# Reading the moving operand of the three-product matmuls from its two halves in turn

## The chip, the cores and the metric

The kernel runs on one core of one Trainium2 chip. The metric is the device time of one execution in microseconds (us), taken as the median over several runs. A profile is one execution recorded by the hardware profiler; its span goes from the first to the last instruction.

## The reference

A decoder trunk of two layers on a residual stream x of 256 tokens by 1024 channels, all in float32. What the change touches are the big weight products: the feed-forward layers' input and output projections, the combined input projection of the token mixer, the projections of its three branches and its output projection.

```python
def _swiglu(h, w_in, w_out):
    gate, up = jnp.split(h @ w_in, 2, axis=-1)
    return (jax.nn.silu(gate) * up) @ w_out
...
for l in range(DEPTH):
    mod = (c_act @ ada_w[l] + ada_b[l]).reshape(bsz, 3, 3, D_MODEL)
    h = _modulated_norm(x, norm_g[l, 0], mod[:, 0, 0], mod[:, 0, 1])
    x = x + MACARON_WEIGHT * mod[:, 0, 2][:, None, :] * _swiglu(h, ffn1_w_in[l], ffn1_w_out[l])
    h = _modulated_norm(x, norm_g[l, 1], mod[:, 1, 0], mod[:, 1, 1])
    mix = _token_mixer(h, positions, mix_w_in[l], ...)
    x = x + mod[:, 1, 2][:, None, :] * mix
    h = _modulated_norm(x, norm_g[l, 2], mod[:, 2, 0], mod[:, 2, 1])
    x = x + MACARON_WEIGHT * mod[:, 2, 2][:, None, :] * _swiglu(h, ffn2_w_in[l], ffn2_w_out[l])
return _rms_norm(x, final_norm_g)
```

Here D_MODEL is 1024 and the feed-forward width is 2816.

## The kernel before

Activations lie transposed: channels on the 128 partitions, the 256 tokens along the free dimension. So every big product has a block of 128 by 128 weights as the stationary operand (the one that TensorE holds) and a strip of 128 channels by 256 tokens as the moving operand (the one that streams through), and its result is 128 output channels by 256 tokens in PSUM, half a bank.

The products are done in float32r, a rounded form of float32. To keep precision, each float32 operand is split into a rounded high part and the rest as a low part, and a product is taken as three: weights high by activations high, weights high by activations low, weights low by activations high. All three add into the same PSUM place. This is `mm3` (lines 1417 to 1421), and its three matmuls are lines 1419, 1420 and 1421 in the profile. It is called by `in_tile` (input projections), by `out_slot` (output projections) and by the branch projections.

Weights come from memory in slots of 2048 columns per partition. SyncE's queue loads a slot into one of the four places of `raw`; ScalarE rounds it into `wh` (line 547); VectorE subtracts to get `wl` (line 868); TensorE uses the slot and counts `w_used` up, on which ScalarE waits to write that slot's place again. `wh` and `wl` have two places each. The activations' parts are `hh` and `hl` (in the profile h_hi and h_lo), `hidh` and `hidl` (hid_hi, hid_lo) for the feed-forward's hidden values, `yh` and `yl` (y_hi, y_lo) for the branches. Gaps are laid between tensors, so that `wh` and `wl` start 128 bytes past a multiple of 512 bytes, and the activations' parts 64 bytes past one.

Other matmuls don't go through `mm3`: `first_slot` (lines 1431, 1433, 1437) takes a stage's first slot in an order of its own, and `tok_mm` (lines 1479 to 1481) has the activations stationary and the weights moving, in one block with 256 columns and in another with 128. The mixer's small matmuls (heads, transposes at line 1731, the solver at line 1824) are in full float32. `fill` puts `mm3` tiles of the gates' projections between them, so that TensorE has work while the other engines prepare.

The order on each engine is the order in which the code is written; waits on semaphores tie the engines together.

Of the kernel before, what the change touches and what calls it, by code (L numbers as in the profile page):

```python
# [173 lines left out]
def hybrid_trunk(nc, a, per_layer, tally):  # L174
    out_dram = a["out"]
    ctx = ExitStack()
    with ctx:
# [1236 lines left out]
        def _(pe):  # L1414
            M = nc.tensor.matmul

            def mm3(out, wsl, rhs_h, rhs_l, start, stop):

                M(out, wh[(slice(None),) + wsl], rhs_h, start=start, stop=False, skip_group_check=True)  # L1419
                M(out, wh[(slice(None),) + wsl], rhs_l, start=False, stop=False, skip_group_check=True)  # L1420
                return M(out, wl[(slice(None),) + wsl], rhs_h, start=False, stop=stop, skip_group_check=True)  # L1421
# [19 lines left out]
            def in_tile(s, half, b, col, n=P):  # L1441

                for k in range(KD):
                    w0 = (half * KD + k) * n
                    last = mm3(PS[0:n, b, col:col + T], (s % 2, slice(w0, w0 + n)), hh[:, k, :], hl[:, k, :],
                               k == 0, k == KD - 1)
                return last
# [4 lines left out]
            def out_slot(n, s, first, last_, rows, l, o):  # L1452


                def product(k, c, start, stop):
                    w0 = k * D + c * P
                    return mm3(out_block(n, c), (s % 2, slice(w0, w0 + P)), *rows(k), start, stop)

                if last_:

                    split_ready(s, 1, o, l)
                    for c in range(KD):
                        product(0, c, False, False)
                        ins = product(1, c, False, True)
                        if c in (1, 3, 5, 6):
                            ins.then_inc(*one("out_done"))
                    ins.then_inc(*one("w_used"))
                    return
                for k in range(2):
                    split_ready(s, k, o, l)  # L1470
                    for c in range(KD):
                        ins = product(k, c, first and k == 0 and c in (0, 2, 4, 6, 7), False)
                ins.then_inc(*one("w_used"))
# [60 lines left out]
            for l in range(DEPTH):  # L1534
# [168 lines left out]
                def fill(parts):  # L1703


                    for part in range(filled[0], filled[0] + parts):
                        j, half, k0 = part // 4, part // 2 % 2, part % 2 * (KD // 2)
                        s = GATE_IN + j
                        if part % 4 == 0 and j >= 2:
                            pe.wait_ge(*at("gate_ready", j - 1, l))  # L1710
                        if k0 == 0:
                            split_ready(s, half, still, l)
                        for k in range(k0, k0 + KD // 2):
                            w0 = (half * KD + k) * P
                            ins = mm3(PS[:, 5 + j % 2, half * T:(half + 1) * T], (s % 2, slice(w0, w0 + P)), hh[:, k, :],
                                      hl[:, k, :], k == 0, k == KD - 1)
                        if part % 4 == 3:
                            ins.then_inc(*one("w_used"))
                    filled[0] += parts
# [108 lines left out]
                for tt in range(TT):  # L1828
                    n = 7 * tt
# [98 lines left out]
                for kb in range(9):  # L1928
                    n, k = kb // 3, kb % 3
# [7 lines left out]
                    for c in range(KD):  # L1937
                        b = BR_BANKS[n] + c // 2
# [99 lines left out]
```

## Time and profile before

| | |
|---|---|
| median of 3 runs | 1378.35 us (1373.07 to 1393.77) |
| profiled execution, its own time | 1366.5 us |
| its span | 1364.7 us |
| mean granted TensorE clock | 0.997 |
| TensorE busy (matmul) | 1293.5 us, 95% of the span |
| TensorE busy (weight load) | 1258.8 us, 92% |
| VectorE, ScalarE, GpSimd busy | 933.4, 632.6, 239.7 us |

The profile gives a row to every instruction. A matmul instruction has two: a weight load (PEld), and the matmul itself (PE). Rows of matmuls overlap, since the next begins before the one before has ended; what a matmul costs in a dense stretch is therefore the time from one start to the next, not the length of its row.

### The profile page before, as it was taken

To read this page: it belongs to the slowest core of one execution; us is meant where nothing else is said; L and a number is where in the kernel's file an instruction comes from. 1 tells how busy PE (TensorE), PEld (TensorE's weight loads), DVE (VectorE), ACT (ScalarE), POOL (GpSimd) and SP (SyncE) were. 2 spreads that over 40 slices of the span, in tenths; PEclk is the share of its full clock that TensorE was granted. 3 is DMA by queue.
4 is the path that set the end of the run, shared out by engine and by line. 5 is a ranking of instruction groups with operands and counts; after the bars stand their busy time and mean duration, and the time that the engine had idled before them with its cause. 6 is when DMAs were issued, how large, how long until landed. Compare 5 with 4: busy or idle time off the path is not lost.

```text
span 1364.7 us, 30015 instructions
## 1 busy us (share of the span) xinstructions
PE 1293.5 (95%) x12966; PEld 1258.8 (92%) x12966; DVE 933.4 (68%) x1324; ACT 632.6 (46%) x913; POOL 239.7 (18%) x265
## 2 busy tenths in 40 slices
PE   2999999999899999999999999999999999999998
PEld 1999998988789999999999999998879999999997
DVE  6777678676756776666676776776765478667655
ACT  2544445566524455444354443547553344644433
POOL 1233440001020001332013331000103000123300
PEclk9999999999999999999999999999999999999999
DMA  9987975515103746776768887662430175577762
GB/s 362 360 295 281 314 282 189 227 47 216 63 4 137 302 166 248 276 289 236 280 233 291 295 312 262 250 247 66 179 127 4 64 294 185 213 261 295 276 219 93
DMA packets 65137, 298.25 MB, mean 219 GB/s; under 512 B 9218, under 2 KB 10242, under 8 KB 47747
## 3 DMA queue, kind: packets, MB, share of 16 engines
q1 hardware_dynamic: 65026, 296.69, 59.3%
q8 instruction: 81, 1.33, 0.4%
q14 instruction: 30, 0.24, 0.0%
HBM read 295.62 MB, written 1.05 MB: 217 GB/s over the span
## 4 chain that ended last, share of the span: by engine, by line
PE 85%; DVE 7%; ACT 4%; DMA 1%; issue 1%; DVEq 1%; ACTq 0%; SPq 0%
PE PS L1419 24%; PE PS L1420 24%; PE PS L1421 24%; PE PS L1824 3%; DVE wl L868 2%; PE PS L1491 1%; DVE scr L894 1%; PE PS L1640 1%; DVE h_lo L887 1%; DMA raw<-in_ada_w 1%; DVE raw L954 1%; PE PS L1431 1%; PE PS L1437 1%; DMA ada_w_ring<-in_ada_w 1%; PE PS L1480 1%
## 5 line engine op out<-in xcount | busy, mean ns | idle before, releaser
L868 DVE TENSOR_TENSOR wl<-raw,wh 128x1024 fp32r<-128x1024 f32 (+1 forms) x400 | 470.2, 1215 | 288.3 <-ACT wh L547 288.1
L547 ACT ACTIVATE wh<-raw 128x1024 fp32r<-128x1024 f32 (+1 forms) x400 | 396.9, 1039 | 474.2 <-PE PS L1421 430.8
L1419 PE MATMUL PS<-h_hi,wh 128*128 128x256 f32 x2160 | 603.3, 279 | 10.8 <-DVE wl L868 6.6
L1420 PE MATMUL PS<-h_lo,wh 128*128 128x256 f32 x2160 | 598.3, 277 | 0.0
L1421 PE MATMUL PS<-h_hi,wl 128*128 128x256 f32 x2160 | 598.2, 277 | 0.0
L1419 PEld LDWEIGHTS PS<-h_hi,wh 128*128 128x128 f32 x2160 | 406.3, 188 | 16.3 <-issue 10.8
L1420 PEld LDWEIGHTS PS<-h_lo,wh 128*128 128x128 f32 x2160 | 406.7, 188 | 0.2
L1421 PEld LDWEIGHTS PS<-h_hi,wl 128*128 128x128 f32 x2160 | 406.6, 188 | 0.0
L1421 PE MATMUL PS<-hid_hi,wl 128*128 128x256 f32 x704 | 194.3, 276 | 0.0
L1419 PE MATMUL PS<-hid_hi,wh 128*128 128x256 f32 x704 | 194.3, 276 | 0.0
L1420 PE MATMUL PS<-hid_lo,wh 128*128 128x256 f32 x704 | 194.3, 276 | 0.0
L954 DVE SCALAR_TENSOR_TENSOR ada_w_ring<-ada_w_ring,c_row 128x1024 f32<-128x1024 f32 x154 | 186.8, 1218 | 10.8 <-ACT c_row L608 7.0
L1325 POOL CAST hid_hi<-hf 128x256 fp32r<-128x256 f32 x88 | 96.1, 1092 | 366.1 <-DVE hf L937 366.1
L1419 PEld LDWEIGHTS PS<-hid_hi,wh 128*128 128x128 f32 x704 | 132.1, 188 | 0.0
L1420 PEld LDWEIGHTS PS<-hid_lo,wh 128*128 128x128 f32 x704 | 132.1, 188 | 0.0
L1421 PEld LDWEIGHTS PS<-hid_hi,wl 128*128 128x128 f32 x704 | 132.1, 188 | 0.0
L1333 POOL TENSOR_TENSOR scr<-scr 128x256 f32<-128x256 f32 x14 | 11.5, 824 | 383.2 <-ACT scr L565 383.0
L1327 POOL TENSOR_TENSOR hid_lo<-hf,hid_hi 128x256 fp32r<-128x256 f32 x88 | 65.2, 741 | 12.7 <-issue 0.2
L1393 POOL TENSOR_TENSOR rw_m<-scr 128x256 f32<-128x256 f32 x24 | 18.0, 770 | 175.3 <-ACT scr L639 79.6
L1431 PE MATMUL PS<-h_hi,wh 128*128 128x256 f32 x96 | 27.1, 302 | 20.6 <-ACT h_hi L580 20.6
L1407 POOL TENSOR_TENSOR A_X<-A_T,cst 128x384 f32<-128x384 f32 x20 | 23.2, 1175 | 109.1 <-DVE A_T L1185 88.2
L1431 PEld LDWEIGHTS PS<-h_hi,wh 128*128 128x128 f32 x96 | 19.9, 208 | 22.0 <-issue 22.0
(284 smaller groups left out, 1402.3 us busy)
## 6 DMA issues: line engine op xcount, KB each, us to landing
raw<-in_ffn_w_in SPq DMA_DIRECT2D x88, 1024.0 KB, 5.6
ada_w_ring<-in_ada_w SPq DMA_DIRECT2D x154, 512.0 KB, 5.1
raw<-in_mix_w_in SPq DMA_DIRECT2D x46, 1024.0 KB, 6.0
raw<-in_ffn_w_out SPq DMA_DIRECT2D x44, 1024.0 KB, 5.8
raw<-in_branch_w SPq DMA_DIRECT2D x8, 1024.0 KB, 9.5
raw<-in_mix_w_out SPq DMA_DIRECT2D x8, 1024.0 KB, 4.9
raw<-in_ada_w SPq DMA_DIRECT2D x6, 512.0 KB, 10.8
raw<-in_mix_w_in SPq DMA_DIRECT2D x4, 512.0 KB, 3.6
```

The lines of the kernel that those rows point to most:

```text
L547: nc.scalar.activation(wh[:, s % 2, h * n:(h + 1) * n], raw[:, s % 4, h * n:(h + 1) * n], ACT.Copy).then_inc(*one("w_hi"))
L868: V.tensor_tensor(wl[:, s % 2, h * n:(h + 1) * n], raw[:, s % 4, h * n:(h + 1) * n], wh[:, s % 2, h * n:(h + 1) * n].bitcast(F32), ALU.sub ...
L954: V.scalar_tensor_tensor(place, place, 1.0, crow[:, :], ALU.mult, ALU.mult, accum_out=adac[:, col:col + 1]).then_inc(*inc("ada_used"))
L1325: G.tensor_copy(dh, hf[:, j % 2, :])
L1327: G.tensor_tensor(dl, hf[:, j % 2, :], dh.bitcast(F32), ALU.subtract).then_inc(*one("hid_ready"))
L1393: G.tensor_tensor(m[:, c, :], pb[:, e % 2, i, 0:T], pb[:, e % 2, i, 1:T + 1], ALU.subtract).then_inc(*one("shift_d"))
L1407: G.tensor_tensor(X[tt], AT[tt], chunk_mask(LEVELS[b]), ALU.mult).then_inc(*one("X_ready"))
L1419: M(out, wh[(slice(None),) + wsl], rhs_h, start=start, stop=False, skip_group_check=True)
L1420: M(out, wh[(slice(None),) + wsl], rhs_l, start=False, stop=False, skip_group_check=True)
L1421: return M(out, wl[(slice(None),) + wsl], rhs_h, start=False, stop=stop, skip_group_check=True)
L1431: M(ps, wh[:, s % 2, w0:w0 + P], hh[:, k, :], start=(k == 0 and half == 0), stop=False, skip_group_check=True)
L1824: ins = M(PS[half(q), b, o:o + 64], lhs[half(q), par, c, :], rhs[half(q), par, c, :], start=True, stop=True)
```

## The change

`mm3` reorders the 256 columns of its moving operand and of its result. Columns are seen as two halves (a) of four runs (b) of 32 columns (n) each, and are taken in the order b, a, n: run 0 of the first half, run 0 of the second half, run 1 of the first half, and so on. With 4 bytes a column, a run is 128 bytes, and the two halves lie 512 bytes apart. The result is written by the same pattern, so each column lands where it landed before. The stationary operand is read as before. No instruction is added, taken away or moved, and no wait changes; `first_slot`, `tok_mm` and all other matmuls stay as they were.

```diff
--- before.py
+++ after.py
@@ -1414,8 +1414,13 @@
         def _(pe):
             M = nc.tensor.matmul
 
+            def turns(t):
+
+                return t.rearrange("p (a b n) -> p b a n", a=2, n=32)
+
             def mm3(out, wsl, rhs_h, rhs_l, start, stop):
 
+                out, rhs_h, rhs_l = turns(out), turns(rhs_h), turns(rhs_l)
                 M(out, wh[(slice(None),) + wsl], rhs_h, start=start, stop=False, skip_group_check=True)
                 M(out, wh[(slice(None),) + wsl], rhs_l, start=False, stop=False, skip_group_check=True)
                 return M(out, wl[(slice(None),) + wsl], rhs_h, start=False, stop=stop, skip_group_check=True)
```

The changed kernel has the same 7165 rows in TensorE's order as the kernel before, one for one; in the rows of `mm3` the operand's form goes from 128x256 to 128x4x2x32, and its three lines become 1424 to 1426.

## Rows read from the trace of the kernel before

**Rows 1.** The page, part 1: busy time, share of the span, instructions; part 2, the TensorE clock.

```profile
PE 1293.5 (95%) x12966; PEld 1258.8 (92%) x12966; DVE 933.4 (68%) x1324; ACT 632.6 (46%) x913; POOL 239.7 (18%) x265
...
PEclk9999999999999999999999999999999999999999
```

**Rows 2.** The page, part 4: the chain that ended last, by engine and by line.

```profile
PE 85%; DVE 7%; ACT 4%; DMA 1%; issue 1%; DVEq 1%; ACTq 0%; SPq 0%
PE PS L1419 24%; PE PS L1420 24%; PE PS L1421 24%; PE PS L1824 3%; DVE wl L868 2%; PE PS L1491 1%; DVE scr L894 1%; PE PS L1640 1%; DVE h_lo L887 1%; DMA raw<-in_ada_w 1%; DVE raw L954 1%; PE PS L1431 1%; PE PS L1437 1%; DMA ada_w_ring<-in_ada_w 1%; PE PS L1480 1%
```

**Rows 3.** The page, part 5: groups by line; busy, mean ns, idle before and its releaser.

```profile
L1419 PE MATMUL PS<-h_hi,wh 128*128 128x256 f32 x2160 | 603.3, 279 | 10.8 <-DVE wl L868 6.6
...
L1419 PE MATMUL PS<-hid_hi,wh 128*128 128x256 f32 x704 | 194.3, 276 | 0.0
```

**Rows 4.** The same groups for the mixer's y tiles, from all groups by line.

```profile
L1419 PE MATMUL PS<-y_hi,wh 128*128 128x256 f32 x144 | 39.7, 276 | 0.0
```

**Rows 5.** Timeline of the feed-forward stage: start us, us it lasts, engine, line, operands.

```profile
149.91 0.28 PE L1419 MATMUL PS<-h_hi,wh 128*128 128x256 f32 x1
149.91 0.19 PEld L1420 LDWEIGHTS PS<-h_lo,wh 128*128 128x128 f32 x1
150.02 0.28 PE L1420 MATMUL PS<-h_lo,wh 128*128 128x256 f32 x1
150.03 0.19 PEld L1421 LDWEIGHTS PS<-h_hi,wl 128*128 128x128 f32 x1
150.14 0.28 PE L1421 MATMUL PS<-h_hi,wl 128*128 128x256 f32 x1
150.14 0.19 PEld L1419 LDWEIGHTS PS<-h_hi,wh 128*128 128x128 f32 x1
```

**Rows 6.** Ends of the timeline from 150 to 160, TensorE alone, and that window's own row.

```profile
149.80 0.28 PE L1421 MATMUL PS<-h_hi,wl 128*128 128x256 f32 x1
...
160.00 0.28 PE L1421 MATMUL PS<-hid_hi,wl 128*128 128x256 f32 x1
...
150.00:160.00 10.00, 10.00 (x91) 1.00 0.81 281
```

**Rows 7.** Ends of the timeline at the mixer's output projection, TensorE alone, and its window.

```profile
485.16 0.36 PE L1419 MATMUL PS<-h_hi,wh 128*128 128x256 f32 x1 [1.31 <-DVE h_lo L1265]
485.35 0.28 PE L1420 MATMUL PS<-h_lo,wh 128*128 128x256 f32 x1
...
496.19 0.28 PE L1419 MATMUL PS<-h_hi,wh 128*128 128x256 f32 x1
...
485.30:496.30 11.00, 11.00 (x94) 1.00 0.51 191
```

**Rows 8.** Timeline of the value projection with 128 moving columns; 48 instructions from 246.94 on.

```profile
246.94 0.22 PE L1479 MATMUL PS<-wh,h_hi 128*128 128x128 f32 x1
247.00 0.28 PE L1480 MATMUL PS<-wh,h_lo 128*128 128x128 f32 x1
...
252.14 0.28 PE L1481 MATMUL PS<-wl,h_hi 128*128 128x128 f32 x1
```

**Rows 9.** Timeline of nine full-precision transposes of 128 columns, merged in one row.

```profile
324.26 1.15 PE L1731 MATMUL PS<-cst,mla_s 128*128 128x128 f32 x9
...
L1731 PE MATMUL PS<-cst,mla_s 128*128 128x128 f32 x36 | 5.0, 276 | 0.0
```

**Rows 10.** Timeline of the shortest matmuls, 64 columns each, merged in one row.

```profile
374.07 1.58 PE L1824 MATMUL PS<-A_inv,A_X 64*64 64x64 f32 x48
```

**Rows 11.** Waits: who waited for whom, us in total, times, longest.

```profile
ACT wh L547 <- PE PS L1421: 430.8, 141, 4.3
DVE wl L868 <- ACT wh L547: 288.1, 159, 4.7
```

**Rows 12.** Windows: PE, PEld, DVE, ACT, POOL busy (instructions), clock, DMA share, GB/s.

```profile
34.00:68.00 34.00, 31.46 (x259) 31.50 (x260) 25.93 (x44) 17.75 (x25) 7.85 (x8) 1.00 0.95 360
68.00:102.00 34.00, 34.00 (x303) 34.00 (x302) 24.36 (x32) 14.13 (x20) 11.75 (x12) 1.00 0.85 294
```

## The prediction

> **What bounds the kernel now.** I read the page's busy times and clock first [rows 1]: TensorE is busy 95% of the span, its weight loads 92%, no other engine over 68%, and the granted clock is 2.4 GHz almost throughout. The chain of waits says the same in another way: 85% of it is TensorE, and the three lines of `mm3` alone hold 24% each, 72% together [rows 2]. The waits show the other engines behind TensorE and not ahead of it: ScalarE waits 430.8 us for TensorE to give back a place of `wh`, and VectorE's split follows ScalarE [rows 11]. So a nanosecond won or lost per `mm3` matmul goes nearly whole into the time. The exception is the start: from 34 to 68 us the DMA engines are 95% busy at 360 GB/s and only 259 matmuls run, against 303 in the next window of the same length [rows 12].
>
> How many matmuls are they? The groups by line give 2160 on h, 704 on the hidden values and 144 on y for each of the three lines [rows 3, 4], so 3 x 3008 = 9024.
>
> What does one cost? The row's own length, 0.28 us, is of no use, since rows overlap; the distance of starts counts. In the feed-forward stage 91 matmuls start from 149.80 to 160.00 [rows 6]: 10.20 us over 90 distances are 113.3 ns. 9024 x 113.3 ns = 1022 us, three quarters of the span, as the chain says.
>
> **What sets the 113.3 ns** decides everything here, because the change touches only the stream of the moving operand and of the result. In the timeline each weight load starts with, or 0.01 us after, the matmul before it, and the next matmul starts 0.11 us later [rows 5]. So two things run side by side in each interval: 256 moving columns pass, and the next 128 weight columns are loaded. Whichever is later sets the pace. Three stretches tell them apart.
>
> First, `tok_mm` with only 128 moving columns and the same 128 weight columns: matmuls number 2 to 48 start from 247.00 to 252.14 [rows 8], 5.14 us over 46 distances, 111.7 ns. Half as many moving columns save 1.6 ns. That speaks for the weight load as the bound, with the moving stream beside it. (It isn't proof: this form may take more than one clock a column.)
>
> Second, nine float32 transposes take 1.15 us, the last of them about 0.276 us [rows 9]: (1.15 - 0.276) / 8 = 109 ns. It is the shortest pace of a full weight load in this trace, and I take it as the floor: 4.1 ns below `mm3`.
>
> Third, the same `mm3` has a slower pace too. At the mixer's output projection 93 matmuls start from 485.35 to 496.19 [rows 7] (the window's 94, less the one at 485.16): 10.84 us over 92 distances, 117.8 ns, at the same clock. The instructions, tiles and starts of tiles are of the same kind as in rows 6. Something in how the two streams meet costs 4.5 ns more there, and the pace holds for the whole stretch. So the pace is not fixed by counts of columns alone.
>
> By the Trainium skill's page "TensorE: Matmul & The Clock Gate" (Part 2, step 1, on LDWEIGHTS) the moving operand and the weights are read through two independent ports of SBUF, and a weight load takes nothing from a running matmul; by that rule the order in which moving columns are read could change nothing, and both rivals of pace below would have no chance. The two paces of rows 6 and 7 keep me from trusting it fully.
>
> **The change part by part.** Instructions, waits, queue entries and bytes: none added, removed or moved, so nothing of the sum comes from there. The stationary side is as before. What is new in each of 9024 matmuls is seven jumps in the reading address and seven in the writing address, between eight runs of 32 columns, and another order in which the moving stream passes the places of a partition.
>
> The jumps: no row of this trace has a TensorE operand in several runs, so I bound them. From below, nothing beyond the pace itself, for as many columns pass as before. From above, by the shortest matmuls here: 48 of 64 columns in 1.58 us [rows 10], less about 0.22 us for the last, are 28.9 ns each; if every run of 32 columns cost as much as such a matmul, one `mm3` matmul would take 231 ns and the kernel 9024 x 118 ns = 1062 us more. I take nothing, for a run is no instruction and has no weight load or start of its own, and because the moving stream has some room beside the weight load: about the 4.1 ns between 109 and 113.3, or 0.6 ns a jump.
>
> The order: from below, the pace falls to the 109 ns of rows 9: 9024 x 4.1 ns = 37 us less, of which about 1 us is lost in the first 68 us where DMA decides, so 36 us. From above, the pace of rows 7 everywhere: 9024 x 4.5 ns = 41 us more, less what already runs so, about 40 us. I take nothing here either, since rows 8 put the pace on the weight load, whose own order doesn't change. Half of the lower end is a case too: the 111.7 ns of rows 8 would bring 9024 x 1.6 ns = 14 us, 1.1%.
>
> The sum is 0 on the profiled execution's 1366.5 us. That execution lies 11.9 us below the median of the three runs, 1378.35 us; differences are put on the median. Forecast: 1378 us, the pace stays at 113.3 ns.
>
> **The rivals.** A measurement of this kernel can tell about 2%, 27.6 us, from no change; over 9024 matmuls that is 3.06 ns each. Cases A to D:
>
> A, the weight load alone sets the pace: 1378 us, its own range 1363 to 1392 (the half gain of 14 us, or as much lost). 0.45.
>
> B, the moving read disturbs the weight read before, and no longer after. In 256 columns the moving stream goes through 1024 bytes while the weight load goes through 512, so with a plain order it overtakes once a matmul; with the halves in turn both advance by 512 bytes a matmul, and it needn't overtake. If that meeting is the 4.1 ns above the floor, the time is 1378 - 36 = 1342 us. For it: 109, 111.7, 113.3 and 117.8 ns for the same weight load. Against it: rows 8, where half the moving columns still take 111.7 ns. It decides from 110.3 ns down. 0.27.
>
> C, the other side: in turns, the fast stream runs ahead over 128 bytes, jumps back, and passes the weight read up to four times instead of once, at each block of 128 bytes. The pace of rows 7 then becomes the rule in all `mm3` stretches: 1378 + 40 = 1418 us. It decides from 116.4 ns up. For it: that pace exists, and holds once it is there; against it: it is rare now, and I can't say what brings it on. 0.20.
>
> D, the jumps are paid: above the room of 4.1 ns, at more than (4.1 + 3.1) / 7 = 1.0 ns a jump, the time is over 2% longer; at 2 ns a jump the pace is 109 + 14 = 123 ns and the time 1378 + 9024 x 9.9 ns = 1467 us. 0.08. The Trainium skill's page "PSUM — Partial Sum Buffer" (Specifications) says that any access pattern that isn't contiguous slows matmuls significantly, with lines of 8 bytes. Taken as it stands it is this rival. A run of 32 columns fills 16 such lines whole, so only the bare wording speaks against the change; no row here tests it.
>
> That the change doesn't reach the chip's instructions is excluded, since the order of the changed kernel carries the form 4x2x32 at these lines.
>
> **How the numbers follow.** The chances are those of the cases: faster by over 2% 0.27 (B), within 2% 0.45 (A), slower by over 2% 0.28 (C and D). The range for 8 in 10 has to hold A, B and C: from 1378 - 42 (B, with some stretches that are at 117.8 ns brought down too) = 1336 to 1378 + 42 = 1420 us. It leaves out D and the tails of B and C, some 0.12.
>
> **What the profile of the changed kernel would show.** The distance of starts in the feed-forward stage decides: 113 ns for A, 109 to 111 for B, about 118 for C, over 120 for D. In B and C ScalarE's wait for TensorE moves the same way, since ScalarE's own work stays: less of the 430.8 us in B, more in C. The start of weight loads beside matmuls tells which stream is late: if the next load starts with each matmul and the matmul follows it at once, the load still leads; if matmuls start long after their load is done, the moving stream has become the bound. VectorE and ScalarE rows should keep their lengths. The forecast would be wrong if either stream hinders the other in SBUF or PSUM in a way that depends on addresses, in whichever direction.

## The result, and the profile after

The changed kernel takes 1409.83 us (median of 4 runs, 1408.28 to 1410.37) against 1379.21 us (4 runs, 1373.07 to 1393.77): slower by more than the 2% that count as clear. The ratio is 1.0267, with a 95% interval of 1.0218 to 1.0316; ratios here and below leave out slow executions (over 1.5% above the fastest of the same kernel, here the one at 1393.77 us), and the two medians by themselves give 1.0222. The four runs of the changed kernel lie within 2.1 us of each other, those of the kernel before within 20.7; that turned out to be a clue.

The profiled execution took 1408.28 us, 41.8 us more in span than the profiled one before. The page of the changed kernel, part 1, the TensorE clock of part 2, and some groups of part 5:

```profile
span 1406.5 us, 30015 instructions
PE 1338.1 (95%) x12966; PEld 1303.4 (93%) x12966; DVE 933.3 (66%) x1324; ACT 633.9 (45%) x913; POOL 239.9 (17%) x265
...
PEclk9999999999999999999999999999999999999999
...
L1424 PE MATMUL PS<-h_hi,wh 128*128 128x256 f32 x2160 | 612.5, 284 | 7.8 <-DVE wl L868 3.5
L1426 PE MATMUL PS<-h_hi,wl 128*128 128x256 f32 x2160 | 607.5, 281 | 0.0
...
L1424 PEld LDWEIGHTS PS<-h_hi,wh 128*128 128x128 f32 x2160 | 406.8, 188 | 13.5 <-issue 10.1
...
L1424 PE MATMUL PS<-hid_hi,wh 128*128 128x256 f32 x704 | 198.0, 281 | 0.0
```

Against [rows 1, 3]: the same count of instructions, the same clock, VectorE, ScalarE and GpSimd as long as before to within 1.3 us, weight loads of 188 ns as before. TensorE's matmul rows alone are longer, by 4 to 5 ns each.

The timeline of TensorE in the feed-forward stage, first and last row from 150 to 160, and that window's row:

```profile
149.83 0.28 PE L1426 MATMUL PS<-h_hi,wl 128*128 128x256 f32 x1
...
159.93 0.28 PE L1424 MATMUL PS<-h_hi,wh 128*128 128x256 f32 x1
...
150.00:160.00 10.00, 10.00 (x86) 1.00 0.88 315
```

86 starts in place of 91 [rows 6]: 10.10 us over 85 distances are 118.8 ns. Over the whole trace the mean distance of starts within `mm3` is 118.8 ns, before it was 113.7 (the stretches at 113.3, but for the one of [rows 7] at 117.8). 9024 x 5.1 ns = 46 us; the span grew by 42. Part of the rest is in the group's idle time, which fell from 10.8 to 7.8 us: a slower TensorE waits less for weights. ScalarE's wait for TensorE grew, as the prediction said it would if the pace fell back:

```profile
ACT wh L547 <- PE PS L1426: 470.2, 141, 4.5
DVE wl L868 <- ACT wh L547: 325.5, 160, 4.8
```

against 430.8 and 288.1 us [rows 11].

### The profile page after: what moved, and what is told of

Same layout as the page of the kernel before. It is cut to its first block, busy times and chain, and to the rows that moved or that the text cites. A ratio compares the mean times of both kernels' runs of the same rounds, so it can differ in the third digit from the quotient of the medians.

```text
span 1406.5 us, 30015 instructions
## 1 busy us (share of the span) xinstructions
PE 1338.1 (95%) x12966; PEld 1303.4 (93%) x12966; DVE 933.3 (66%) x1324; ACT 633.9 (45%) x913; POOL 239.9 (17%) x265
## 4 chain that ended last, share of the span: by engine, by line
PE 86%; DVE 7%; ACT 3%; DMA 1%; issue 1%; DVEq 1%; ACTq 0%; SPq 0%
PE PS L1424 24%; PE PS L1426 24%; PE PS L1425 24%; PE PS L1829 3%; DVE wl L868 2%; PE PS L1496 1%; DMA ada_w_ring<-in_ada_w 1%; PE PS L1645 1%; PE PS L1442 1%; PE PS L1436 1%; DMA raw<-in_ada_w 1%; PE PS L1438 1%; DVE scr L894 1%; PE PS L1486 1%; PE PS L1485 1%
## 5 line engine op out<-in xcount | busy, mean ns | idle before, releaser
L1424 PE MATMUL PS<-h_hi,wh 128*128 128x256 f32 x2160 | 612.5, 284 | 7.8 <-DVE wl L868 3.5
L1426 PE MATMUL PS<-h_hi,wl 128*128 128x256 f32 x2160 | 607.5, 281 | 0.0
L1425 PE MATMUL PS<-h_lo,wh 128*128 128x256 f32 x2160 | 607.4, 281 | 0.0
L1424 PE MATMUL PS<-hid_hi,wh 128*128 128x256 f32 x704 | 198.0, 281 | 0.0
L1425 PE MATMUL PS<-hid_lo,wh 128*128 128x256 f32 x704 | 198.0, 281 | 0.0
L1426 PE MATMUL PS<-hid_hi,wl 128*128 128x256 f32 x704 | 198.0, 281 | 0.0
L1436 PE MATMUL PS<-h_hi,wh 128*128 128x256 f32 x96 | 27.6, 307 | 20.9 <-ACT h_hi L580 20.9
## 6 DMA issues: line engine op xcount, KB each, us to landing
raw<-in_ada_w SPq DMA_DIRECT2D x6, 512.0 KB, 10.8
```

The lines of the kernel that those rows point to most:

```text
L1436: M(ps, wh[:, s % 2, w0:w0 + P], hh[:, k, :], start=(k == 0 and half == 0), stop=False, skip_group_check=True)
```

## The experiments

All paces below are distances of starts in a dense stretch, worked out as above.

### Reading or writing?

**e1_read** turns only the moving operands, **e2_write** only the result.

```diff
-                out, rhs_h, rhs_l = turns(out), turns(rhs_h), turns(rhs_l)
+                rhs_h, rhs_l = turns(rhs_h), turns(rhs_l)        # e1_read
+                out = turns(out)                                 # e2_write
```

> The changed kernel with only the two moving operands read in turns; results are written in plain order, so that their columns land permuted and the output is another one. The trace of the changed kernel has a start every 118.8 ns in the three-product matmuls, before it was 113.3 to 113.7. Theory READ (the new order of the moving read meets the weight read more often): the pace stays near 118.8 ns and the time near 1408 us. Theory WRITE (the jumps in the result's address cost): the pace falls back to 113.3 to 113.7 ns, the time to about 1367 us. Theory JUMPS (each side's seven jumps cost their share): about 116 ns.

> The other half alone: moving operands read in plain order, results written in runs of 32 columns of two halves in turn, so that columns land permuted and the output is another one. READ: back at 113.3 to 113.7 ns and about 1367 us. WRITE: 118.8 ns and about 1408 us. JUMPS: about 116 ns.

e1_read took 1410.98 us, e2_write 1385.56, the kernel before on the same chip 1372.61 (one run each). The timelines, e1_read from 150 to 160 with its window:

```profile
149.81 0.28 PE L1425 MATMUL PS<-h_lo,wh 128*128 128x256 f32 x1
...
159.90 0.28 PE L1426 MATMUL PS<-h_hi,wl 128*128 128x256 f32 x1
...
150.00:160.00 10.00, 10.00 (x86) 1.00 0.86 298
```

10.09 us over 85 distances, 118.7 ns: reading in turns alone gives the whole loss, as theory READ expected. And e2_write, from 150 to 160 and from 530 to 540:

```profile
150.00:160.00 10.00, 10.00 (x91) 1.00 0.77 277
...
529.78 0.28 PE L1425 MATMUL PS<-h_lo,wh 128*128 128x256 f32 x1
...
539.91 0.28 PE L1424 MATMUL PS<-h_hi,wh 128*128 128x256 f32 x1
...
530.00:540.00 10.00, 10.00 (x87) 1.00 0.85 312
```

`mm3` runs in four long feed-forward stretches of 1536 matmuls each (the expectation further down counts 1534). The first is at the old 113.3 ns (91 starts); the second is at 117.8 ns, 10.13 us over 86 distances, and so are the third and the fourth, each to its end. Both are paces of the kernel before [rows 6, 7]; no stretch is at 118.8. READ had expected 1367 us, and the time is 19 us over that. So e2_write isn't "half the loss", as its 13 us over the run before might suggest: it is the old pair of paces, with more stretches at the slower one. Whether the turned write makes the slower one more likely, this single run can't say; in TensorE alone, below, the write changes nothing.

### How many jumps?

```diff
-                return t.rearrange("p (a b n) -> p b a n", a=2, n=32)
+                return t.rearrange("p (a b n) -> p b a n", a=2, n=64)
```

> The changed kernel with runs of 64 columns in place of 32: three jumps per matmul in place of seven. If each jump costs its share of the 5.1 ns between 113.7 and 118.8, the pace is 113.7 + 5.1 x 3/7 = 115.9 ns and the time 9024 x 2.9 ns = 26 us under 1408. If the order in which the two reads pass each other decides, the pace is no straight line in the number of jumps; with half as many returns of the moving read it could be anywhere from 113 to 119 ns.

e3_n64 took 1387.63 us. Its mean pace was 115.9 ns, just what three of seven jumps should cost. That agreement was false: the trace has no stretch at 115.9, only stretches at 113.3 and at 117.8. Here are the windows of its first and its fourth feed-forward stretch:

```profile
150.00:160.00 10.00, 10.00 (x88) 1.00 0.85 298
1250.00:1260.00 10.00, 10.00 (x91) 1.00 0.74 281
```

So I ran the same kernel twelve times more.

> Halves in turn, in runs of 64 columns, timed in rounds. Its single look gave 1387.6 us with two paces in one trace: 113.3 ns in some dense stretches and 117.8 in others, the long feed-forward stretches of 1534 matmuls among them. The plain order has the same two paces. TWO PACES (a stretch falls into either pace at its start and keeps it to its end, in both kernels): both kernels' runs lie on steps of 1534 x 4.45 ns = 6.8 us over about 1366.5 us, from none to four of them (1366.5, 1373.3, 1380.2, 1387.0, 1393.8), and the ratio is unclear, between 0.995 and 1.015. JUMPS (three jumps cost 26 us in every run): this kernel's runs all lie near 1388 to 1395 us, a ratio of 1.008 to 1.015 with little scatter.

Twelve runs: median 1374.33 us, from 1366.03 to 1387.67; 17 runs of the kernel before beside it: 1374.13, from 1365.34 to 1390.59. The ratio is 1.0015 (0.9975 to 1.0055). Runs of 64 columns cost nothing that these runs can tell, JUMPS is out and TWO PACES fits. The 17 runs of the kernel before lie in heaps: five from 1365.3 to 1367.0, six from 1371.9 to 1374.7, three from 1380.0 to 1381.8, two near 1386, one at 1390.6. The first four heaps lie near the steps of 6.8 us that TWO PACES expects of four feed-forward stretches, each of which falls into one of two paces; the last run, expected at 1393.8, lies 3 us off. The traces agree: with none of the four stretches at 117.8 the profiled executions took 1366.5 us (before) and 1366.61 (the turned one with 64 columns), with three of four 1385.56 (e2_write) and 1387.63 (e3_n64), where 1387.0 is expected. No slower execution of the kernel before itself was traced, so for that kernel it is worked out from times. The changed kernel has a single pace, and its runs lie within 2.1 us.

### TensorE by itself

Does the cost need the rest of the kernel? **m1_pace** has TensorE alone run groups of 96 matmuls, weights high by moving high, high by low, low by high, one form per group:

```python
for W, H in ((wh, hh), (wh, hl), (wl, hh)):
    yield o, W[:, c:c + 128], H[:, k:k + w]
...
for o, w, h in triples(32, 16, 256): mm(o, w, turn(h, 32), **K)  # read only
for o, w, h in triples(32, 16, 256): mm(turn(o, 32), w, h, **K)  # write only
```

The first two arguments are the first columns of the weights and of the moving operand past a multiple of 512 bytes; 32 and 16 columns are the kernel's 128 and 64 bytes. I call the first less the second, in bytes, the distance: 64 in the kernel.

> A measurement by itself, which computes nothing of the reference (it hands the input x back): TensorE alone issues groups of 96 matmuls of the three-product kind, in dense runs with a pause before each, in 25 forms, all of them twice. Weights start 0 to 448 bytes past the moving operand's start modulo 512, in steps of 64, for plain order and for halves in turn; then, at the kernel's places (128 and 64), the moving read alone in turns, the write alone in turns, runs of 64, 16 and 8, and 128 and 512 columns. If the meeting of the two reads in a partition decides, the pace differs between places, and reading alone gives 118.8 ns where writing alone gives 113.3. If the jumps are paid, all eight places give one pace in turns, 118.8 ns, and it rises with the count: runs of 64 about 115.5, of 16 about 125, of 8 above 135. If other engines' work matters, here, with them idle, turned and plain forms agree.

The timeline of m1_pace, the 9th and the 96th matmul of three groups (plain at distance 0, then at the kernel's place reading alone in turns, and writing alone in turns):

```profile
34.04 0.28 PE L89 MATMUL PS<-hh,wl 128*128 128x256 f32 x1
...
44.48 0.28 PE L89 MATMUL PS<-hh,wl 128*128 128x256 f32 x1
...
228.49 0.28 PE L121 MATMUL PS<-hh,wl 128*128 128x256 f32 x1
...
238.83 0.28 PE L121 MATMUL PS<-hh,wl 128*128 128x256 f32 x1
...
240.65 0.28 PE L123 MATMUL PS<-hh,wl 128*128 128x256 f32 x1
...
250.51 0.28 PE L123 MATMUL PS<-hh,wl 128*128 128x256 f32 x1
```

Over 87 distances: 10.44 us are 120.0 ns, 10.34 are 118.9, 9.86 are 113.3. Reading alone has the whole cost and writing alone none, as in the whole kernel. The other forms, in the same way, each the same in both passes to 0.1 ns:

| distance in bytes | 0 | 64 | 128 | 192 | 256 | 320 | 384 | 448 |
|---|---|---|---|---|---|---|---|---|
| plain, ns | 120.0 | 113.3 | 118.7 | 117.8 | 120.0 | 113.3 | 118.7 | 117.8 |
| turns of 32, ns | 119.0 | 118.8 | 120.0 | 120.0 | 118.9 | 118.8 | 120.0 | 120.0 |

At distance 64: turns of 64 columns 113.3, of 16 120.0, of 8 123.4; a price for each jump would have given 115.5, 125 and over 135. So no other engine is needed; the distance of the two operands in a partition and the order of the read set the pace, and both rows repeat after 256 bytes. The change's gain or loss depends on that distance: in TensorE alone, turns of 32 gain 1 ns at 0 and lose 5.5 at 64.

### Distance or absolute place?

> Again TensorE alone, nothing of the reference computed (x is handed back), 43 forms of 96 matmuls each. The first such run gave, in plain order, 120.0, 113.3, 118.7 and 117.8 ns with the weights 0, 64, 128 and 192 bytes past the moving operand's place, the same again from 256 on, and in turns of 32 columns 119.0, 118.8, 120.0 and 120.0. Here the steps are 16 bytes; some forms move the moving operand's place instead of the weights'; 512 columns and stationary blocks of 32 and 64 columns are there as well. MEETING (two reads of one partition hinder each other, by their distance in bytes modulo 256): moving the other operand by d gives what the weights moved by 256 - d gave (64: 117.8, 128: 118.7, 192: 113.3), both moved by 64 gives 120.0, and with a weight load of only 32 columns, plain and in turns cost the same, near 109 ns. ADDRESS (the absolute place of the weights or of the moving operand alone counts): moving the moving operand leaves 120.0 or follows a rule of its own. STREAM (the turned stream is slow by itself): with 32 weight columns it stays at 118.8 against 113.3.

With the moving operand moved instead of the weights (m2_places, plain):

| moving operand moved by | 64 | 128 | 192 | both moved by 64 |
|---|---|---|---|---|
| pace, ns | 117.8 | 118.6 | 113.3 | 120.0 |

That is the row above read at 192, 128, 64 and 0: the distance counts, not the place. In steps of 16 bytes, plain, from 0 to 240: 120.0, 118.3, 118.4, 117.8, **113.3**, 118.8, 118.6, 120.1, 118.7, 120.0, 120.0, 118.1, 117.8, 116.7, 117.8, 117.4. Only 64 gives 113.3. Turns of 64 columns gave 120.0, 113.3, 118.7 and 117.8 at 0, 64, 128 and 192, the plain row again. Turns of 32 repeated the table's 119.0, 118.8 and 120.0, but at 192 they gave 118.7 where m1_pace had 120.0: this one place isn't set by the distance alone.

Other shapes follow other rules. With 512 moving columns the plain pace was 226.8, 233.3, 232.3 and 228.9 ns at 0, 64, 128 and 192, so there 64 is the worst of the four and not the best. With 64 weight columns it was 119.1 ns at distance 64 (120.0 in turns). And with 32 weight columns it was 113.3 ns plain and 118.3 in turns: MEETING had expected about 109 for both, and failed there; STREAM had expected this.

Does the whole kernel follow? **e4_same_place** is the kernel before with the distance at 0, **e6_turn_d32** the changed kernel with the distance at 32.

```diff
-        phase("h_gap", 64)
-        base = (base + 511 - 64) // 512 * 512 + 64
+        phase("h_gap", 128)                              # e4_same_place; 96 in e6_turn_d32
+        base = (base + 511 - 128) // 512 * 512 + 128     # the same
```

> The kernel before, plain order, with the activations' parts (and all that lies in the shared region) moved from 64 to 128 bytes past a multiple of 512, where the weights' parts start too: distance 0 in place of 64. By the run of TensorE alone the plain pace there is 120.0 ns and has no second value: MEETING expects a pace of 120.0 ns in the three-product matmuls and 9024 x (120.0 - 113.7) = 57 us over the profiled 1366.5, about 1423 us. If distance matters only with the other engines idle, the pace stays at 113 to 118 ns, 1367 to 1395 us.

> The changed kernel, halves in turn by 32 columns, with the activations' parts and the shared region moved to 96 bytes past a multiple of 512, so that the weights start 32 bytes further on in place of 64. TensorE alone gave 117.8 ns there against 118.8 at 64. MEETING: a pace of 117.8 ns and 1408.3 - 9024 x 1.0 ns = 1399 us. If the pace were the turns' alone: 118.8 ns and 1408 to 1410 us.

e4_same_place took 1420.18 us (1423 expected), 54 more than the profiled execution before and 46 more than the median of the 17 runs, for two shifted starts and no other edit. Its timeline from 150 to 160:

```profile
149.83 0.28 PE L1419 MATMUL PS<-h_hi,wh 128*128 128x256 f32 x1
...
159.91 0.28 PE L1419 MATMUL PS<-h_hi,wh 128*128 128x256 f32 x1
...
150.00:160.00 10.00, 10.00 (x85) 1.00 0.98 339
```

10.08 us over 84 distances, 120.0 ns, as TensorE alone had it. e6_turn_d32 took 1398.69 us, where 1399 were expected and 1409.83 is the changed kernel: 87 starts from 150 to 160, 10.13 us over 86 distances, 117.8 ns. This kernel too has two paces. Its windows in the first and the second feed-forward stretch:

```profile
150.00:160.00 10.00, 10.00 (x87) 1.00 0.87 327
550.00:560.00 10.00, 10.00 (x88) 1.00 0.46 174
```

The second is at 116.7 ns (10.15 us over 87 distances), and so is the third; that makes 117.2 over the whole trace. TensorE alone hadn't shown 116.7 there, so the close hit of 1399 is in part luck.

### Which stream sets the pace?

> TensorE alone once more, 41 forms of 96 matmuls, nothing of the reference computed. So far the pace depends on the distance of weights and moving operand in bytes, modulo 256, and yet a weight load of only 32 columns (its row 108 ns long in place of 188) left the pace where it was: 113.3 plain, 118.3 in turns. Here the stationary block has 8 columns, at 16 distances plain and four in turns, 32 columns at four and four, and the count of moving columns goes from 128 to 512 with 8 and with 128 weight columns. LOAD LENGTH (the two reads hinder each other as long as both run): with 8 weight columns all distances and both orders come near 109 ns, and 512 columns near 216. LOAD START (one collision at the head of each load, however short): the paces at 8 columns follow those at 128, 120.0, 113.3, 118.7, 117.8. STREAM (the moving read has a pace of its own beyond 2.4 GHz a column): with 8 columns 113.3 at every distance, 119 in turns at every distance, and the time rises by more than 0.417 ns a column from 256 to 512.

Timeline of m3_small_load, the 9th and 96th matmul: 8 weight columns with 128 moving columns, then with 256, plain, at distance 64:

```profile
132.84 0.22 PE L101 MATMUL PS<-hh,wl 128*8 128x128 f32 x1
...
138.06 0.22 PE L101 MATMUL PS<-hh,wl 128*8 128x128 f32 x1
...
149.11 0.28 PE L105 MATMUL PS<-hh,wl 128*8 128x256 f32 x1
...
158.97 0.28 PE L105 MATMUL PS<-hh,wl 128*8 128x256 f32 x1
```

60.0 ns and 113.3 ns. The first number settles [rows 8]: 128 moving columns need only 60 ns, so the 111.7 ns there (m3_small_load has 111.7 again with 128 weight columns) are indeed the weight load. The second overturns what I made of it: 256 moving columns take 113.3 ns with almost no weight load beside them, more than the load's 111.7. No group of 256 moving columns in any run, whatever its weights, was below 113.3, so the 109 ns of [rows 9] weren't to be had in this form; 512 columns took 231.1 (LOAD LENGTH had 216).

The same trace shows that the prediction's sign for the later stream, a load that starts with each matmul, doesn't tell the two apart. Here the load lasts 0.09 us of 0.113, can't be the bound, and starts with the matmul all the same, as in [rows 5]:

```profile
155.12 0.28 PE L105 MATMUL PS<-hl,wh 128*8 128x256 f32 x1
155.12 0.09 PEld L105 LDWEIGHTS PS<-hh,wl 128*8 128x8 f32 x1
155.23 0.28 PE L105 MATMUL PS<-hh,wl 128*8 128x256 f32 x1
```

In turns of 32 with 8 weight columns the paces are 117.8, 116.7, 117.8 and 116.7 ns at 0, 64, 128 and 192. So STREAM held mostly, but not alone: the turned read is slower with hardly a load beside it, and a full load adds 1 to 3 ns. Over all runs, the ten groups in turns of 32 with 8 or 32 weight columns lie between 116.7 and 118.7 ns, while 16 of the 23 plain ones are at 113.3. And the short load isn't harmless: plain with 8 columns was at 113.3 for 12 of 16 distances from 0 to 480 and at 115.6 to 120.0 for the other four. Nor does the rule of 256 bytes hold there: 113.3 ns at 64, 120.0 at 320. The same form at 64, 113.3 here, was at 116.7 in the next run (below). With 8 weight columns there are several paces for one form, so these numbers bound the stream's own share and don't fix it.

### Jumps, or places passed twice?

A turn of 32 columns has seven jumps, and it also goes through each 128 bytes of the 256 twice in a row. **m4_orders** separates the two. "matched" jumps as often, or more, but always to the place modulo 256 bytes that comes next in plain order; "twice" reads one run again before going on.

```python
def matched(t, k, n):
    return t.rearrange("p (s u n) -> p s u n", s=k, n=n)[:, :, 0:4 * k:k, :].rearrange("p s u n -> p u s n")
def twice(t, n):
    return t.rearrange("p (b n) -> p b n", n=n).unsqueeze(2).broadcast_to([P, 128 // n, 2, n])
```

> TensorE alone, 33 forms of 96 matmuls, only the order of the moving read differs, results are written plainly and nothing of the reference is computed. A moving stream with 8 weight columns beside it ran at 113.3 ns plain and 116.7 to 117.8 in turns of 32, so the turned read has a slower pace of its own, to which a full weight load adds 1 to 3 ns. Runs of 64 columns, which are 256 bytes, gave the plain pace at all four distances. PLACE (what counts is the sequence of places modulo 256 bytes that the read goes through): eight runs of 32 and sixteen runs of 16 that jump by whole 256s plus the next place (matched32, matched16) give the plain pace, 113.3 ns at a distance of 64 and 120.0 at 0, whatever the count of jumps; reading one run of 32 twice before going on (twice32) gives what turns of 32 give, 118.8 ns, and twice64 gives 113.3. JUMPS (each jump shorter than 64 columns costs): matched32 is at 118.8, matched16 at 120.0 like turns of 16, and stay32 (eight runs, all at the same place modulo 256) at 118.8 as well.

Timeline of m4_orders at distance 64 with 128 weight columns, 9th and 96th matmul: turns of 32 (L112), matched in eight runs of 32 (L118), matched in sixteen of 16 (L120), each run of 32 twice (L126):

```profile
57.33 0.28 PE L112 MATMUL PS<-hh,wl 128*128 128x256 f32 x1
...
67.67 0.28 PE L112 MATMUL PS<-hh,wl 128*128 128x256 f32 x1
...
94.41 0.28 PE L118 MATMUL PS<-hh,wl 128*128 128x256 f32 x1
...
104.27 0.28 PE L118 MATMUL PS<-hh,wl 128*128 128x256 f32 x1
...
106.10 0.28 PE L120 MATMUL PS<-hh,wl 128*128 128x256 f32 x1
...
115.96 0.28 PE L120 MATMUL PS<-hh,wl 128*128 128x256 f32 x1
...
142.40 0.28 PE L126 MATMUL PS<-hh,wl 128*128 128x256 f32 x1
...
152.74 0.28 PE L126 MATMUL PS<-hh,wl 128*128 128x256 f32 x1
```

118.9, 113.3, 113.3 and 118.9 ns. Fifteen jumps cost nothing if the place modulo 256 bytes goes on as in plain order; seven jumps that repeat the place cost 5.5 ns, and as much when the repeated run is the very same columns. Runs of 64 read twice gave 113.3, staying at one place for all eight runs 120.0, and both matched forms at distance 0 gave 120.0, the plain value there. PLACE held at every form with full weights, and JUMPS is out there. With 8 weight columns it isn't so clean: matched in eight runs of 32 gave 113.3, but in sixteen of 16 120.0, the same as turns of 16, and plain 116.7.

## Why the prediction was wrong

The forecast was 1378 us with the pace unchanged; the time of rival C came true, nearly at its price (1418 forecast, 1410 measured). The stated range, up to 1420, held the result only because C was in it.

**Right.** That `mm3`'s pace decides and TensorE is the bound: 5.1 ns per matmul came back as 42 us of span. That nothing else moves: VectorE's and ScalarE's rows kept their lengths. The count of 9024. That the jumps and the write cost nothing (against D): m1_pace shows it for the write, m4_orders for the jumps of the read with full weights.

**The step that failed** is in "What sets the 113.3 ns": "That speaks for the weight load as the bound, with the moving stream beside it." [rows 8] show what the load needs, 111.7 ns, and it is true that the load sets the pace there (TensorE alone took 111.7 with 128 moving columns, and 60.0 once the load was short). But I had no row for what 256 moving columns need without a load and assumed about 109 ns from full-precision transposes; measured they need 113.3. The stream on which the change works was the later of the two already, by 1.6 ns, and had none of the 4.1 ns of room that the forecast counted on. An order that slows the moving read, to 116.7 or more even with a short load, shows at once.

**Also failed, the step from which A took its weight:** "I take nothing here either, since rows 8 put the pace on the weight load, whose own order doesn't change." The pace of full weights isn't the load's alone: with both orders unchanged, e4_same_place shifted the starts and went from 113.3 to 120.0 ns. Plain order at the kernel's distance of 64 bytes is the one good case among the sixteen distances tried; turning the read leaves it.

**B** rested on the picture that in plain order the moving read overtakes the weight read once a matmul at a cost of 4.1 ns. At the kernel's distance plain order with full weights costs no more than the stream with 8 weight columns (113.3 both), so there was nothing to win. At distance 0, where plain order takes 120.0, turns gain 1 ns in TensorE alone, B's direction but a quarter of its size.

**C's picture and size.** That C came true is in part luck. In its picture the moving read jumps back and passes the weight read up to four times. But the matched orders jump at least as often and cost nothing (113.3), and the turned read is slow with 8 weight columns too. For its size, C took the slower pace of [rows 7], 117.8 ns, for all stretches. The pace is another one, 118.8, so in the profile the loss is 42 us and not 40. In the medians it is 31 us; going by its times, the kernel before has one or more of its feed-forward stretches at 117.8 in most runs, where its profiled execution had none, and I took that for the rule. The pace of [rows 7] was no rare case of the mixer: in e2_write and e3_n64 three of the four long stretches have it.

The Trainium skill's rule of two independent read ports ("TensorE: Matmul & The Clock Gate", Part 2, step 1) isn't what these runs show: shifting where the weights or the moving operand start, with all else kept, moved the pace between 113.3 and 120.0 ns with full weights. The wording of the Trainium skill's page "PSUM — Partial Sum Buffer" (Specifications), that any write which isn't contiguous slows matmuls, isn't borne out either for runs of 32 columns: m1_pace has 113.3 ns with and without.

**Open:** what brings a stretch of the kernel before into 113.3 or 117.8 ns at its start (TensorE alone, after a pause, was at 113.3 all nine times that a group in plain order with full weights ran at distance 64 modulo 256); and the mechanism inside the memory. The runs show, for full weights and 256 columns, a rule in distances modulo 256 bytes and in repeated places; whether it is the two reads that collide, or the stream with itself in part, they show only in so far as the turned read is slow with 8 weight columns too.

## What to carry to other kernels

When a change alters how an operand is read, ask what its stream needs alone, not only which of two parallel streams a trace row seems to show as the later; a few groups of the bare instruction on the idle engine answer that in one run. With float32r matmuls of 128 weight and 256 moving columns, treat the distance between the starts of weights and moving operand modulo 256 bytes as a parameter: it was worth up to 6% of a matmul's pace, and 46 to 54 us in this kernel. Measure it anew for another shape, for with 512 columns the order of the distances was another. Keep reads in an order that goes through those 256 bytes evenly. Before a mean pace is explained by a fraction (three jumps of seven), look whether any stretch has that pace.

## What the runs showed of the hardware

- The pace of 128 by 128 weights with 256 moving float32r columns at 2.4 GHz depends on the distance of the operands' starts modulo 256 bytes: 113.3 ns at 64, 116.7 to 120.1 at the other fifteen steps of 16. In the whole kernel, 64 and 0 are 1366.5 and 1420 us in the profiled executions. With 512 columns, 0 is the best of four distances (226.8 ns) and 64 the worst (233.3).
- 256 moving float32r columns take 113.3 ns at best, with 8 weight columns beside them as with 128; with 8, 128 take 60.0 and 512 take 231.1: about 0.44 to 0.47 ns a column, more than the 0.417 of one column a clock at 2.4 GHz.
- With full weights, the order of the read costs by the places modulo 256 bytes that it repeats, not by its jumps (118.8 ns against 113.3 at distance 64); the write in runs of 32 columns costs nothing (113.3).
- Plain order at distance 64 has a second stable pace, 117.8 ns, which a stretch keeps for up to 1536 matmuls (e2_write, e3_n64). Four such stretches of 6.8 us would make up most of the 25 us scatter of the kernel before. Turns of 32 at distance 32 have two as well, 117.8 and 116.7 ns.
